# Two-layer encoder trunk on 8 cores: expert weights rounded to bf16 in DRAM during the mixers, loaded from there on SyncE's queue, which also gives the tile tokens

## The reference

```python
# layer 0: pooling mixer (512 columns) + chunked attention (8 heads of 64, own chunk of 64 + 8 before it)
h = h + concat(pool_mixer(p), chunk_attention(q, k, v, rel_bias)) @ w_out      # p,q,k,v = rmsnorm(h) @ w_in
h = h + hier_moe(rmsnorm(h), layer 0)
# layer 1: gMLP gating over blocks of 128 positions
h = h + (u * (tril(w_s) @ layernorm(v) + b_s)) @ w_out                        # u,v = gelu(rmsnorm(h) @ w_in + b)
h = h + hier_moe(rmsnorm(h), layer 1)
return rmsnorm(h)

def hier_moe(h):        # 4 groups of 4 experts, D_EXPERT = 256
    g = top-1 group of h @ wg_router;  the 2 best of its 4 experts by we_router
    combine = softmax weight of the group * softmax over the two experts
    return sum over the two experts of (silu(h @ w_gate) * (h @ w_up) * combine) @ w_down
```

## Time and profile before

| | us |
|---|---|
| median of 3 runs (lowest, highest) | 2281.47 (2276.26, 2308.52) |
| the profiled execution's own time | 2270.85 |
| its span, slowest core (core 0) | 2269.3 |
| spans of the eight cores | 2238.6 to 2269.3 |
| busy PE, DVE, ACT, POOL | 1790.8, 1258.0, 966.0, 585.9 |
| DMA queue of POOL (q0): MB, share of 16 engines | 130.45, 27.3% |
| DMA queue of SP (q1): MB, share of 16 engines | 106.66, 14.4% |

### The profile page before, as it was taken

One profiled execution on the slowest core, in us unless ns is written; L12 is line 12 of the kernel. 1 busy time (PEld: TensorE's weight loads), 2 busy tenths in 40 slices (PEclk: granted clock), 3 DMA queues, 4 the chain that ended last, 5 costly groups with the idle time before them and its releaser, 6 DMA issues.

```text
span 2269.3 us, 39155 instructions; the slowest of 8 cores (2238.6 to 2269.3 us)
## 1 busy us (share of the span) xinstructions
PE 1790.8 (79%) x10530; PEld 942.6 (42%) x10530; DVE 1258.0 (55%) x2625; ACT 966.0 (43%) x1579; POOL 585.9 (26%) x821
## 2 busy tenths in 40 slices
PE   2798988988988039676898399999999339788996
PEld 1344444544444015333454155555555214343453
DVE  1756466466463445343564366666666266555776
ACT  1565565565554014222343264555444105344554
POOL 2111011111011304323333112111111204544664
PEclk9999999999997559888899699999999659999998
DMA  9621321321111773879631933333322443957310
GB/s 200 131 73 47 94 87 46 102 66 38 64 58 47 127 140 120 155 152 180 172 110 29 238 107 103 104 97 99 99 78 75 93 112 99 199 131 166 132 66 2
DMA packets 96985, 240.51 MB, mean 106 GB/s; under 512 B 28960, under 2 KB 41632, under 8 KB 96032
## 3 DMA queue, kind: packets, MB, share of 16 engines
q0 software_dynamic: 58704, 130.45, 27.3%
q1 hardware_dynamic: 37968, 106.66, 14.4%
HBM read 257.15 MB, written 91.36 MB: 154 GB/s over the span
## 4 chain that ended last, share of the span: by engine, by line
PE 63%; DMA 12%; DVE 9%; issue 7%; ACT 4%; POOL 2%; POOLq 1%; DVEq 0%; SPq 0%; ACTq 0%
PE psum L739 14%; PE psum L761 7%; DMA arena<-scr,arena 6%; PE psum L908 5%; PE psum L489 5%; PE psum L1010 5%; PE psum L1140 5%; PE psum L1173 4%; PE psum L1123 4%; PE psum L984 3%; PE psum L918 2%; PE psum L483 2%; DMA arena<-grow 2%; DMA wc<-ab_in 2%; PE psum L971 1%
## 5 line engine op out<-in xcount | busy, mean ns | idle before, releaser
L739 PE MATMUL psum<-wc,arena 128*128 x1760 | 416.4, 392 | 39.6 <-POOLq L682 35.1
L739 PEld LDWEIGHTS psum<-wc,arena 128*128 128x128 bf16 x1760 | 173.2, 100 | 237.5 <-issue 66.9
L657 POOL DMA_INDIRECT arena<-scr,arena x110 | 129.5, 1178 | 412.1 <-DVE arena L766 186.2
L761 PE MATMUL psum<-wc,arena 128*128 x880 | 218.6, 393 | 12.2 <-issue 4.0
L732 ACT ACTIVATE arena<-psum 128x1024 bf16<-128x1024 bf16 x110 | 112.5, 1023 | 245.5 <-PE psum L731 239.4
L766 DVE TENSOR_TENSOR arena<-psum,arena 128x512 f32<-128x512 f32 x220 | 152.2, 692 | 93.9 <-PE psum L761 74.1
L744 DVE SCALAR_TENSOR_TENSOR arena<-psum,arena 128x256 bf16<-128x256 f32 x220 | 105.2, 482 | 175.6 <-ACT arena L743 148.4
L908 PE MATMUL psum<-arena,wc 128*128 128x512 bf16 x768 | 201.0, 394 | 0.0
L974 ACT ACTIVATE arena<-psum 128x1024 bf16<-128x1024 f32 (+1 forms) x240 | 160.9, 702 | 88.0 <-PE psum L971 59.2
L743 ACT ACTIVATE arena<-psum 128x256 f32<-128x256 f32 x220 | 84.3, 383 | 267.7 <-PE psum L739 222.3
L725 DVE SCALAR_TENSOR_TENSOR arena<-arena 128x1024 bf16<-128x1024 f32 x110 | 140.6, 1279 | 102.8 <-DMA arena<-scr,arena 102.4
(11 more groups left out here) (247 smaller groups left out, 3091.1 us busy)
## 6 DMA issues: line engine op xcount, KB each, us to landing
wc<-moe_w POOLq DMA_DIRECT2D x96, 512.0 KB, 25.2
arena<-x SPq DMA_DIRECT2D x64, 512.0 KB, 3.9
scr<-arena SPq DMA_DIRECT2D x64, 512.0 KB, 3.1
arena<-scr SPq DMA_DIRECT2D x64, 512.0 KB, 3.6
wc<-ab_in POOLq DMA_DIRECT2D x8, 512.0 KB, 20.8
arena<-sg_in POOLq DMA_DIRECT2D x4, 1024.0 KB, 22.2
arena<-grow SPq DMA_DIRECT2D x4, 512.0 KB, 24.1
wc<-ab_out POOLq DMA_DIRECT2D x2, 1024.0 KB, 15.0
```

The costliest lines, as they stand in the source:

```text
L657: A("pool", lambda e: e.indirect_dma_start(out=hg[:, s, :], out_offset=None, in_=src[:, :], in_offset=bass.IndirectOffsetOnAxis(ap=idx[:, ...
L739: r = e.matmul(bank(q), lhsT=xT[i][:, kc, :], rhs=wsl(t, q, kc), start=(kc == 0), stop=(kc == 7))
L761: r = e.matmul(bank(b), lhsT=aT[i][:, f, :], rhs=wsl(t, f // 2, c), start=(f == 0), stop=(f == 3))
```

## The change: what it does

- A DRAM tensor `mwb` holds all expert weights in bf16. During each mixer `convert` gives 48 DMAs, DRAM to DRAM, from POOL's queue, each of which rounds one chunk (1 MB read, 0.5 MB written); each waits for the one but one before it. The planner may not place the k-th earlier than 80 + 13 k us (layer 0) or 45 + 8.5 k us (layer 1) in its own time.
- The weight loads read `mwb`, need no cast, and stand on SP's queue. For layer 1 group 0's load has the due number of stage 3 instead of stage 1 and waits for its chunks in `mwb`.
- Tokens and reloads move from POOL's queue to SP's. A reload now goes over ten tiles instead of six, by the list `ASK`, one chunk on eight of them and two on two, and on each of the ten SP waits for the last matmul of `down(t-1)`. Behind it SP reads the table once more, for the case that the group has fewer tiles than ten, and then comes `token(t+1)`.

```diff
+    mwb = nc.dram_tensor("mwb", [2, 4, NCH, 128, 2048], BF16, kind="Internal").ap()
...
-            return e.dma_start(out=wc[c][:, (g % 2) * 2048:(g % 2) * 2048 + 2048], in_=moe_d[l, g, c])
+            return e.dma_start(out=wc[c][:, (g % 2) * 2048:(g % 2) * 2048 + 2048], in_=mwb[l, g, c])
...
-                A("pool", lambda e, c=c: wdma(e, l, g, c), writes=[WK[(l, g % 2, c)]], grp=gr)
+                A("sync", lambda e, c=c: wdma(e, l, g, c), reads=[("mwb", l, g, c)], writes=[WK[(l, g % 2, c)]], grp=gr, nbytes=524288)
+        def convert(l, k):
+            g, c = divmod(k, NCH)
+            gr = P.new_group("cv%d" % (k % 4))
+            A("pool", lambda e: e.dma_start(out=mwb[l, g, c], in_=moe_d[l, g, c]), reads=[("mwb", l) + divmod(k - 2, NCH)] if k >= 2 else [], writes=[("mwb", l, g, c)], grp=gr, nbytes=800000)
...
+            ASK = ((0, 1), (2,), (3,), (4,), (5, 6), (7,), (8,), (9,), (10,), (11,))
...
             def token(t):
                 def fn(e):
-                    v = pload(2 * T + t, 0, 3)
+                    v = vload(SP_T, 2 * T + t, 0, 3)
                     with e.If(v >= 1):
-                        e.wait_ge(P.dsems["w%dg1" % l], 16 * NCH)
-                        for g in (2, 3):
+                        for g in (1, 2, 3):
                             with e.If(v == g):
...
                                 e.wait_ge(P.dsems["w%dg%d" % (l, g)], 16 * NCH)
                     e.free_register(e.to_reg(v))
                     return e.nop()
-                A("pool", fn, reads=[("tab%d" % l, i) for i in (2, 4)], writes=[(pf + "tok", t)]).sem = "tok"
+                A("sync", fn, reads=[("tab%d" % l, 2)], writes=[(pf + "tok", t)]).sem = "tok"
             def reload(t):
                 def fn(e):
-                    v = pload(3 * T + t, 0, 60)
+                    v = vload(SP_T, 3 * T + t, 0, 60)
                     with e.If(v >= 32):
...
-                                    for k in range(6):
-                                        with e.If(v == o + 2 * k):
-                                            if k == 0:
-                                                e.wait_ge(P.sems["pe"], last_pe[t - 1].sigidx)
-                                            for c in (2 * k, 2 * k + 1):
-                                                chunk(e, g, c)
+                                    for k in range(len(ASK)):
+                                        with e.If(v == o + k):
+                                            e.wait_ge(P.sems["pe"], last_pe[t - 1].sigidx)
+                                            ask(e, g, k)
                     e.free_register(e.to_reg(v))
+                    if t + 1 < T:
+                        v = vload(SP_T, 2 * T + t + 1, 0, 3)
+                        with e.If(v >= 2):
+                            for g in (2, 3):
+                                with e.If(v == g):
+                                    r = vload(SP_T, 4 * T + g - 2, 1, len(ASK))
+                                    with e.If(r <= len(ASK) - 1):
+                                        for k in range(1, len(ASK)):
+                                            with e.If(r <= k):
+                                                ask(e, g, k)
...
-            token(0)
+            for t in range(T):
+                token(t)
+                reload(t)
...
+            for k in range(6):
+                P.pr = st * 100.0 + 16 * k; P.nb = 80 + 13.0 * (st * 6 + k)
+                convert(0, st * 6 + k)
...
+                P.pr = st * 100.0 + 16 * k; P.nb = 45 + 8.5 * (st * 6 + k)
+                convert(1, st * 6 + k)
...
-            if st == 1:
-                P.pr = 150.0
+            if st == 3:
+                P.pr = 350.0
                 wbufs(1, 0)
                 wload(1, 0, range(NCH))
```

More of the change, by code:

```diff
@@ L13 @@
 PE_T = mybir.EngineType.PE
-POOL_T = mybir.EngineType.Pool
+SP_T = mybir.EngineType.SP
 D = 1024
@@ L68, in __init__ @@
         self.nseq = 0
+        self.nb = 0.0
         self.span = []
@@ L109, in add @@
         self.nseq += 1
-        op.seq = self.nseq; op.pr = self.pr; op.nbytes = nbytes
+        op.seq = self.nseq; op.pr = self.pr; op.nbytes = nbytes; op.est = self.nb
         if c is None:
@@ L650, in moe @@
             last_pe = {}
+            marks = []
             regs = {}
@@ L659, in gather, with vload, ask @@
                   reads=[("idx", l)] + src_keys, writes=[(pf + "hg", s)], grp=g)
[L661 to L665, removed]
+            def vload(eng, c, lo, hi):
+                return nc.values_load(tab[l][0:1, c:c + 1], engines=[eng], skip_runtime_bounds_check_because="made on the chip from tile starts", min_val=lo, max_val=hi)
+            ASK = ((0, 1), (2,), (3,), (4,), (5, 6), (7,), (8,), (9,), (10,), (11,))
+            def ask(e, g, k):
+                for c in ASK[k]:
+                    wdma(e, l, g, c).then_inc(P.dsems["w%dg%d" % (l, g)], 16)
             def token(t):
                 def fn(e):
-                    v = pload(2 * T + t, 0, 3)
+                    v = vload(SP_T, 2 * T + t, 0, 3)
                     with e.If(v >= 1):
-                        e.wait_ge(P.dsems["w%dg1" % l], 16 * NCH)
-                        for g in (2, 3):
+                        for g in (1, 2, 3):
                             with e.If(v == g):
-                                r = pload(4 * T + g - 2, 2, 12)
-                                with e.If(r <= 10):
-                                    for c in range(2, NCH):
-                                        with e.If(r <= c):
-                                            chunk(e, g, c)
-                                e.free_register(e.to_reg(r))
                                 e.wait_ge(P.dsems["w%dg%d" % (l, g)], 16 * NCH)
@@ L803, in moe @@
                     down(t - 1)
-                reload(t)
-                if t + 1 < T:
-                    token(t + 1)
                 atr(t)
@@ L816, in moe @@
             down(T - 1)
+            for t in marks:
+                last_pe[t].sig = True
             if fin:
@@ L1180, in build_program @@
         for st in range(NS):
+            for k in range(6):
+                P.pr = st * 100.0 + 16 * k; P.nb = 45 + 8.5 * (st * 6 + k)
+                convert(1, st * 6 + k)
+            P.nb = 0.0
             gating(st)
-            if st == 1:
-                P.pr = 150.0
+            if st == 3:
+                P.pr = 350.0
                 wbufs(1, 0)
```

16 lines of the change are left out of this document (9 added, 7 removed).

## The result

| | before | after |
|---|---|---|
| median, us (lowest, highest), 4 runs each | 2278.86 (2269.45, 2308.52) | 2387.40 (2383.66, 2605.57) |
| profiled execution: its time, its span | 2270.85, 2269.3 | 2390.17, 2388.5 |
| lowest and highest span of the eight cores | 2238.6, 2269.3 | 2371.9, 2388.5 |

After by before is 1.0485, 95% interval [1.0434, 1.0536]: 4.9% slower. (The 2605.57 is an execution with one die disturbed; the ratio leaves such ones out.)

The account below looks back on a forecast made before the run. It took PE-bound mixers, and experts losing time to late gathers and tokens, plus the seams. Experts +34 and +56, mixer 1's start -28, seams -4 each, mixers +8: +62 on 2270.85 gives 2333, said as 2340; range 2245 to 2430.

Parts of the forecast that it names:

- The token, the central step: Experts: on 40 reload tiles PE idles 3.8 us for SP's token and loses 1.4 to the clock, 5.2 us a tile.
- Experts: Both layers' experts regions: 438 us against 403.9 (+34) in layer 0, 462 against 405.9 (+56) in layer 1.
- Late gathers gone: Experts: weights leave POOL's queue, so late gathers vanish except 8 us in layer 0 and 5 in layer 1.
- Start of mixer 1: Layer 1's cast loads no longer stand beside gain, biases and rows: -28 us, bounds -16 and -35.
- Mixers: Both mixers: 96 conversions fit the DMA engines, POOL's issues stand before memsets: +8 us, bounds 0 and +68.
- The premise that PE is over 90% busy: Both mixers: little can be won or lost there but by holding PE up.
- Seam into experts 0: Gain row behind 24 chunks lands some 18 us later, multiply and first gather quicker: -4 us, bounds -15 and +15.
- Seam into experts 1: Gain row behind 12 chunks, 19 us, plus its own 3 to 4, against 28.23: -4 us.
- The rival on the held POOL queue: Conversions hold POOL up, memsets and powers behind wait too: +60 on the forecast, 2400 us; chance 0.12.
- The quick SP: Experts: token way 2.0 us or less, clock stays full, 40 tiles cost 80 us instead of 208: 2215; chance 0.11.
- the rival in between: Experts: idle 2.5 to 3 us, clock loss on some tiles, 3.7 us a tile: 2283 us; chance 0.17.
- The late gathers' rival: Experts: gathers stay late despite the move, 35 us left in layer 0: +20, 2360 us; chance 0.10.

Follow-up runs that it names:

- the denser plan: Changed kernel with layer 1's conversions spaced 6.5 us instead of 8.5 and their DMA time halved in the planner's model; 2374.45 us in one run.

## Why the prediction was right, and where not

The forecast was 2340 us, and 2387.40 were measured: inside the range of 2245 to 2430, with the sign and the main cause as said. But by spans +62 was forecast and +119 came. Only half of the growth was foreseen, and the time lies just above the narrower 2300 to 2385 that the forecast gave itself. Of what was missed, 37 us lie in the seam into experts 1, 22 in the experts and 5 in the other seam; the start of mixer 1 gave 5 back.

- **The token, the central step: right, 8% too small.** 5.2 us a tile forecast, 5.6 measured (idle 3.64 for 3.8, clock 1.95 for 1.4). 41 waits and 148 us lie in the 40 and 120 to 170 that were named, and L757 behind them takes 5.0 to 6.5 us on core 1. The two terms err in opposite ways. The mean idle time hides two errors more: the first ask of a layer costs 8.6 and 7.4 us on core 1, not the 4.8 that its steps summed to, and the last asks of a group mostly cost 2.4 to 3.0. Long pauses behind a branch fell into four of core 1's 40 tiles, with 1.7 to 4.1 us, not into one in six with 2.5. The clock was lost on all tiles, not on five of six, and behind waits of 3.5 to 3.9 us `gu` took 5.1 to 6.5 us on that core. Giving the token ahead of the ask, or on POOL's queue, removes most of it.
- **Experts: +34 and +56 forecast, +45.0 and +66.7 measured.** The token is 8 us of the difference in each layer; the rest, some 3 us, was not taken apart.
- **Late gathers gone: right in the list, wrong in the reason.** 8 and 5 us were left in the sum, and no wait for L743 is seen. But the token's idle time covers them. With the token cured 21.9 us are back.
- **Start of mixer 1: -28 forecast, -33.3 measured**, with the tail of experts 0 in it. Right.
- **Mixers: +8 forecast, +6.6 in mixer 0.** The conversions alone measure +2.6 and -0.5. The other builds of the changed kernel, with the same mixer 0, have 753.5 to 757.5 us there, against 758.4 in the changed kernel and 751.8 before, so part of the 6.6 is the spread between executions. The premise that PE is over 90% busy in both mixers is a little off for mixer 0: 563.91 of 635.0 us, 89%, between 110 and 745 us of the trace before. No term hangs on it.
- **Seam into experts 0: -4 forecast, +0.6 measured.** The parts are as said: the gain row 46 us after the mixer's end, multiply 0.69 us. The 24 chunks were issued in 26 us, not 38, and the row landed 19.5 us after its issue, not 3 to 4; that is the 5.
- **Seam into experts 1: -4 forecast, +32.8 measured. This is the step that failed.** I let 12 loads take 19 us by their engine time, as if the engines were free, and I priced the conversions in the mixers alone. On the slowest core the last of them was issued 36 us after mixer 1's end, and the 12 loads took 31 us to be issued. What stood in the forecast as a term of the mixers fell due at the seam, in front of the one load that DVE needs. The run with the gain rows first (67.3 us) and the run with the early conversions (64.6) show that it takes both, the row's place and the late conversions.

The rival on the held POOL queue (2400) is the nearest in number and not in cause: POOL waited for conversions 25.4 us in mixer 0 and 11.0 in mixer 1, and neither mixer grew by it beyond the 6.6 us above; a longer mixer with longer waits of that kind came only with the denser plan. The quick SP (2215) fails with 3.64 us of idle time, and the rival in between (2283, 3.7 us a tile) with 5.6. The late gathers' rival (2360) is half alive: they were late, but under another wait.

## What to carry to other kernels

A wait for the bottleneck engine is best kept on a queue where nothing that this engine needs soon comes behind it. Here the token behind such a wait turned a gain of 3% (2190 us in one run against 2268 in the same comparison) into a loss of 5%, and moving the token cured it. A load that only the next stage's first instruction needs goes first in its queue, ahead of bulk loads, above all where another queue's long packets may still be running. When a wait disappears from the list, ask whether a longer one covers it. When an edit of a planner's number does nothing, look first whether the order changed; and when a part of the change is tried alone, look whether the planner put it in the same place.

## What the runs showed of the hardware

- In the ladder behind an ask the branches on SP follow each other at 0.15 us. But 389 branches of the changed kernel, over eight cores, have a pause of 1.5 to 6 us behind them, and each of these pauses has a packet of the instruction queue in it. The one of 4.1 us at 930.0 met busy DMA engines.
- In the changed kernel each of the 297 waits of 2.2 us or more had `gu` at 4.89 us or longer behind it, up to 6.57. Without the second read the waits of 1.9 to 2.4 us came out both ways, 3.61 and 5.30. The length of a wait alone does not decide it: in the kernel before, 10 of 47 waits of 2.2 us or more had `gu` at 3.61 behind them, one of these a wait of 3.91 us.
- Conversions of 1 MB to 0.5 MB within DRAM land in 7.8 us (median of 46 in mixer 0), at most two at a time, beside PE busy 89% of the time; added to the kernel before, 96 of them left its time as it was (1.0018 [0.9998, 1.0037]).
- A gain row issued behind 24 chunks reaches DVE 19.5 us after its issue, and 6.4 us after it where it stands first in its queue.
- An issue instruction of a chunk on SP, 0.32 us at its shortest, stood for up to 4.5 us in a row of 24 loads with no conversion about, and for 15.7 us while two conversions had most of the engines' time, with no semaphore in play.
- The chain of waits on the page gives SP's queue 3% of the span after the change, although its token costs 148 us: the way there is booked as "issue" (17%). The group's idle time named it.
